# A hybrid decoder layer on one core: two lines for the second row of a pair, mLSTM steps further apart, weight parts shared evenly

## The chip, the core and the metric

The kernel runs on one core of a Trainium2 chip. The metric is the device time of one execution in microseconds; for the kernel before it is the median of three runs.

## What is computed

One inference step of a decoder layer, for a prompt of 2048 tokens (with 16 meta tokens in front) and for 8 samples of 8 tokens, with the same weights. All is float32. Cut to what matters here:

```python
def _in_proj(x, g_pre, w_in, b_in):
    h = _rmsnorm(x, g_pre)
    p = jnp.einsum('btd,dc->btc', h, w_in) + b_in
    return jnp.split(p, ...)          # qa ka va za qm km vm om zm im fm ga gb

def _mlstm_chunk(carry, inp):         # one chunk of 128 tokens, 4 heads of width 256
    Wqk = W * jnp.einsum('blhd,bshd->bhls', q, k)
    num = a[..., None] * jnp.einsum('blhd,bhde->bhle', q, C0) + jnp.einsum('bhls,bshe->bhle', Wqk, v)
    h = num / jnp.maximum(jnp.abs(den), jnp.exp(-m))[..., None]
    C1 = aL[..., None, None] * C0 + jnp.einsum('bshd,bshe->bhde', kw, v)

def _merge(x, att, hm, za, om, zm, ga, gb, w_pa, w_pb, w_out, g_post):
    y_a = att * jax.nn.silu(za)
    y_m = jax.nn.sigmoid(om) * hm * jax.nn.silu(zm)
    merged = jax.nn.sigmoid(ga) * (y_a @ w_pa) + jax.nn.sigmoid(gb) * (y_m @ w_pb)
    return x + _rmsnorm(merged @ w_out, g_post)
```

## The kernel before, in words

**Two stages.** A first stage (up to about 859 us) does the norm, the attention with its projections, and prepares data in DRAM. A barrier follows, and then `stream` runs all other projections; the change is in `stream` and in the last steps of the first stage.

**Passes, tiles, pairs.** `stream` goes through ten passes: ZM, H0 to H3 (one mLSTM head each: its q, k, o and v columns, and that head's mLSTM work), GA, PA, GB, PB and OUT. A pass multiplies 17 tiles of 128 tokens by a 1024x1024 weight. Tile 0 (meta and sample tokens) is a single one with four products; tiles 1 to 16 go in eight pairs (row 0 the odd tile, row 1 the even one) with seven products each, P1, P6, P5, P7, P2, P3, P4 in this order, on sums and differences of operands and of weight blocks (a scheme that saves one product in eight). So a pass has 60 products, and the program counts them through as q. A product is 12 matmuls of 128x512 (line 2760, 2762, 2763: each operand and weight is split into an upper and a lower float32r part). "Step" below is q within a pass, or within a pair from 0 to 6. Three PSUM banks serve all: `bank_x` is bank_first, `bank_y` bank_second, `bank_z` bank_third.

**Results and lines.** VectorE evicts the products (`evict_pair`) into lines of the tile `c`: row 0 of a pair has line 0, row 1 has line 1, the single tile line 2 (`line_of`). P7's eviction makes u3 and then the right half of row 1 (line 2497, semaphore c22), and P3, which uses the same bank, waits for c22. Before it writes into a line, VectorE waits in `wait_line` until the former tile has left it: its store to DRAM (ZM, GA, PA, GB), its mLSTM reads (head passes), its transposes (PB, `transposes`, line 2711), or its last addition (OUT: VectorE norms the row in `norm_row`, line 2555, and POOL adds x in `finish`, line 2215).

**mLSTM steps.** Tile n of a head is turned at q = `turned_at(n)` (TensorE transposes q and k, line 2783), scored one step later (L2792, with the transposes L2772 of the y of the tile before, `y_transposed`), mixed two steps later (L2808, L2809, L2812). ScalarE evicts the transposes (L2342), takes the exponential (L2333) and evicts y (L2379); VectorE makes mx_wqk (L2564) and mx_y (L2622). Tile 0 also does the samples' work inside the product of its mixing (`sample_rows`, L2839) and in the four after it (`state_update`).

**Weights.** A pass uses 28 weight parts ("units" of 128x512). SP loads each into one of `NW` = 6 waiting buffers (L2006), ScalarE makes the upper part (`upper_unit`, L2274), VectorE or POOL the lower (`lower_unit`, L2437 and L2177, `lower_by_dve` decides), two units a step from six steps ahead of a pass to its step 7. Differences of weight blocks for later passes are made on POOL (`differences`, L2184 to L2190) at steps fixed by `DIF_AT`; ScalarE's queue loads them three steps ahead (`load_dif`, L2262, which waits for the store of the one before last) and stores them three steps later (`store_dif`, L2266).

**Order.** Every engine runs a loop over q with its work written in a fixed order, and waits on semaphores. SP asks for the operand of product q + 3 at step q (L1636), and for a head's z four steps ahead of the turn (`load_z`, L2029, which waits for the gates of the tile two before).

## Time and profile before

| | before |
|---|---|
| runs, us | 2915.42, 2923.53, 2921.34 |
| median, us | 2921.34 |
| the profiled execution's own time, us | 2916.61 |
| its span, us | 2914.8 |
| TensorE busy | 2763.5 us, 95% |
| VectorE, ScalarE, POOL busy | 56%, 32%, 26% |
| granted clock of TensorE, mean | 0.979 |

The span runs from the first to the last instruction of one execution. TensorE's granted clock has two levels in the records, 1.00 (2.4 GHz) and 0.50 (1.2 GHz), and a stretch shows their mean. A list of waits says which engine's which line ended the idle time of TensorE; its idle time is the difference of span and busy time.

### The profile page before, as it was taken

The numbers are of one execution on the slowest core, as the hardware profiler recorded it, in microseconds if no ns is written. First come the engines' busy times: TensorE is split into PE (matmuls) and PEld (weight loads), VectorE is DVE, ScalarE is ACT, GpSimd is POOL, SyncE is SP. The second block draws the span as 40 slices with busy tenths as digits, with TensorE's granted clock in tenths as the row PEclk, the third lists the DMA queues.
The fourth block names the chain that finished last, engine by engine and source line by source line (L and its number), as shares of the span: only waits on it lengthen the run. The fifth ranks groups of instructions, "written<-read, shape, count | busy, mean of one in ns | idle before, by whom it ended". The sixth has DMA issues, their size and how long they took to land. (4 is left out here: it accounts for less than half of the span.)

```text
span 2914.8 us, 46458 instructions
## 1 busy us (share of the span) xinstructions
PE 2763.5 (95%) x15620; PEld 2298.4 (79%) x15620; DVE 1636.7 (56%) x4103; ACT 936.0 (32%) x2291; POOL 762.2 (26%) x1064
## 2 busy tenths in 40 slices
PE   6999999999999989999999998999999999999897
PEld 5888888888878768867877886888877878777676
DVE  5775665555652344464455455446256642677766
ACT  5774444444440021131132122113132321433432
POOL 3333534434540021131222223222000010223312
PEclk9999999999999999999999999999999999999999
DMA  8664565455777879887997997989795587856543
GB/s 301 241 214 160 178 210 196 166 176 191 233 232 233 299 250 301 295 305 236 286 309 260 283 284 254 283 278 308 246 304 171 184 301 252 297 186 215 188 147 116
DMA packets 410014, 697.47 MB, mean 239 GB/s; under 512 B 31778, under 2 KB 176551, under 8 KB 409748
## 3 DMA queue, kind: packets, MB, share of 16 engines
q1 hardware_dynamic: 298212, 526.72, 54.9%
q10 hardware_dynamic: 108848, 158.46, 16.1%
q0 software_dynamic: 2720, 9.32, 1.0%
q8 instruction: 128, 2.10, 0.3%
q14 instruction: 106, 0.87, 0.1%
HBM read 526.87 MB, written 169.48 MB: 239 GB/s over the span
## 5 line engine op out<-in xcount | busy, mean ns | idle before, releaser
L2760 PE MATMUL bank_second<-w_all,a_all 128*128 128x512 f32 x736 | 298.9, 406 | 2.0 <-DVE st_u L2491 0.9
L2763 PE MATMUL bank_second<-w_all,a_all 128*128 128x512 f32 x736 | 288.6, 392 | 0.0
L2762 PE MATMUL bank_second<-w_all,a_all 128*128 128x512 f32 x736 | 288.3, 392 | 0.0
L2177 POOL TENSOR_TENSOR w_all<-st_waiting,w_all 128x512 fp32r<-128x512 f32 x59 | 80.1, 1359 | 626.4 <-ACT w_all L2274 626.4
L2342 ACT ACTIVATE mx_qkt<-st_bank_t 128x512 f32<-128x512 f32 x68 | 40.7, 598 | 578.4 <-PE st_bank_t L2783 556.3
L2760 PE MATMUL bank_third<-w_all,a_all 128*128 128x512 f32 x464 | 190.3, 410 | 29.9 <-DVE st_c L2497 12.9
L2760 PE MATMUL bank_first<-w_all,a_all 128*128 128x512 f32 x496 | 197.5, 398 | 4.1 <-DMA a_all<-first_t 2.0
L2763 PE MATMUL bank_first<-w_all,a_all 128*128 128x512 f32 x496 | 194.6, 392 | 0.0
L2762 PE MATMUL bank_first<-w_all,a_all 128*128 128x512 f32 x496 | 194.6, 392 | 0.0
L2274 ACT ACTIVATE w_all<-st_waiting 128x512 fp32r<-128x512 f32 x188 | 111.7, 624 | 246.9 <-PE bank_first L2763 139.2
L307 PE MATMUL bank_first<-w_all,a_all 128*128 128x384 f32 x544 | 189.3, 348 | 0.0
L2184 POOL TENSOR_TENSOR h_raw<-h_raw 128x256 f32<-128x256 f32 x64 | 48.5, 757 | 538.4 <-DMA h_raw<-l_blocks_in 538.2
L2763 PE MATMUL bank_third<-w_all,a_all 128*128 128x512 f32 x464 | 184.6, 398 | 0.0
L2762 PE MATMUL bank_third<-w_all,a_all 128*128 128x512 f32 x464 | 184.4, 397 | 0.0
L309 PE MATMUL bank_first<-w_all,a_all 128*128 128x384 f32 x544 | 182.1, 335 | 0.0
L308 PE MATMUL bank_first<-w_all,a_all 128*128 128x384 f32 x544 | 182.0, 335 | 0.0
L917 ACT ACTIVATE at_sm<-at_sm,at_nmx 128x208 f32<-128x208 f32 x272 | 124.1, 457 | 154.1 <-DVE at_nmx L1138 154.1
L2760 PEld LDWEIGHTS bank_second<-w_all,a_all 128*128 128x128 f32 x736 | 139.6, 190 | 34.5 <-issue 6.8
L2763 PEld LDWEIGHTS bank_second<-w_all,a_all 128*128 128x128 f32 x736 | 139.1, 189 | 30.1
L2762 PEld LDWEIGHTS bank_second<-w_all,a_all 128*128 128x128 f32 x736 | 139.5, 190 | 26.8
L316 PE MATMUL bank_third<-w_all,a_all 128*128 128x256 f32 (+1 forms) x480 | 147.3, 307 | 0.2 <-POOL a_all L297 0.2
L2494 DVE TENSOR_TENSOR st_u<-bank_second,st_t 128x512 f32<-128x512 f32 x80 | 55.2, 690 | 157.3 <-PE bank_second L2763 157.3
(383 smaller groups left out, 7270.6 us busy)
## 6 DMA issues: line engine op xcount, KB each, us to landing
a_all<-sh_t SPq DMA_DIRECT2D x224, 512.0 KB, 5.0
a_all<-hh_t SPq DMA_DIRECT2D x180, 512.0 KB, 5.7
a_all<-hh_t ACTq DMA_DIRECT2D x104, 512.0 KB, 4.8
st_waiting<-difs_t SPq DMA_DIRECT2D x152, 256.0 KB, 6.3
h_raw<-l_blocks_in ACTq DMA_DIRECT2D x64, 512.0 KB, 5.7
difs_t<-h_raw ACTq DMA_DIRECT2D x64, 512.0 KB, 7.3
st_waiting<-l_blocks_in SPq DMA_DIRECT2D x108, 256.0 KB, 6.8
hh_t<-a_all SPq DMA_DIRECT2D x34, 512.0 KB, 6.2
```

Source lines behind the costliest of these rows:

```text
L307: nc.tensor.matmul(out, hi[:, j], k.w_hi[:, j, col:col + n], start=(j == 0), stop=False)
L308: nc.tensor.matmul(out, hi[:, j], k.w_lo[:, j, col:col + n], start=False, stop=False)
L309: last = nc.tensor.matmul(out, lo[:, j], k.w_hi[:, j, col:col + n], start=False, stop=(j == KT - 1))
L316: nc.tensor.matmul(out, hi[:, j], k.w_hi[:, j, col:col + n], start=(j == 0), stop=False)
L917: nc.scalar.activation(sm[:, g, :], sm[:, g, :], ACT.Exp, bias=nmx[:, g:g + 1], scale=HD ** -0.5, accum_out=rs[:, g:g + 1]).then_inc(exp_r ...
L2177: G.tensor_tensor(unit_half(v, 1), unit_view(v), unit_half(v, 0).bitcast(F32), ALU.subtract).then_inc(k.lower_done, 1)
L2184: G.tensor_tensor(d[:, R11], d[:, R12], d[:, R11], ALU.subtract).then_inc(dif_step, 1)
L2274: A.activation(unit_half(v, 0), unit_view(v), ACT.Copy).then_inc(k.upper_done, 1)
L2494: V.tensor_tensor(u3[:, :], bank_y[:, :], t2[:, :] if s in STREAMED else t1[:, :], ALU.add).then_inc(u3_ready, 1)
L2760: T.matmul(bank_view(bank, at), hi, weight_row(k, at, 0, t), start=fresh and t == 0, stop=False, skip_group_check=True)
L2762: T.matmul(bank_view(bank, at), hi, weight_row(k, at, 1, t), start=False, stop=False, skip_group_check=True)
L2763: last = T.matmul(bank_view(bank, at), lo, weight_row(k, at, 0, t), start=False, stop=t == KH - 1, skip_group_check=True)
```

## The change

`line_of` gives row 1 line 1 or 3 by turns, so `c` has four lines, and `former_item` looks two pairs back for row 1; the stores of lines 1 and 3 are counted apart (`stored_count`). In the output pass the norms come one step (row 0) and two steps (row 1) later. `turned_at` puts the turns of a head's tiles 0 to 5 at steps 7, 14, 17, 20, 22 and 25 (before: 4, 11, 12, 16, 18, 23) and those of later even tiles two steps later. `lower_by_dve` gives VectorE two of four lower parts in every pass, where it had three of four in the seven passes behind a streamed one. Four more units of the first pass are loaded in the first stage, into a part of `w_all` that is free then (`staged_unit`), and the ring of waiting buffers begins at `RING`. The semaphore for the right half of tile 0 in the first pass is now incremented by the first stage's own eviction.

```diff
--- before.py
+++ after.py
@@ -71,6 +71,7 @@
 PAIR_SLOTS = 5
+RING = EARLY + 4
@@ -352,6 +353,10 @@
     return k.w_all[:, :, KH * part + kt, 2 * LW:W_COLS]
+
+
+def staged_unit(k, v):
+    return k.w_plain[:, :, v % KH, 2 * LW:W_COLS]
 def unit_part(k, at, part, kt, n):
@@ -651,6 +656,8 @@
                         load_early(e)
+                    for v in range(EARLY, RING):
+                        sp.dma_start(staged_unit(k, v), unit_source(k, v).rearrange("p (i n) -> p i n", i=2)).then_inc(k.staged_in, 16)
                 if t == 0 and a + 1 < KVH:
@@ -1300,7 +1307,7 @@
             V.tensor_tensor(k.h_raw[:, 1, KH:KT].rearrange("p j n -> p (j n)"), k.bank_first[:, :],
-                            k.h_raw[:, 0, KH:KT].rearrange("p j n -> p (j n)"), ALU.add).then_inc(k.first_ready, 1)
+                            k.h_raw[:, 0, KH:KT].rearrange("p j n -> p (j n)"), ALU.add).then_inc(k.c12_ready, 1)
         @block.tensor
@@ -1657,7 +1664,7 @@
 def line_of(g, row):
-    return 2 if is_single(g) else row
+    return 2 if is_single(g) else (0, 1 + 2 * (pairs_before(g) % 2))[row]
 def row_turn(passes, g, row):
@@ -1665,16 +1672,21 @@
     return (N_ITEM - row) * passes.index(g // N_ITEM) + g % N_ITEM + 1 - row
-def stored_count(g):
-
-    n = STORING.index(g // N_ITEM)
-    return 16 * (n + 1 if is_single(g) else (N_ITEM - 1) * n + g % N_ITEM)
+def stored_count(g, row):
+
+    n, i = STORING.index(g // N_ITEM), g % N_ITEM
+    if is_single(g):
+        return 16 * (n + 1)
+    return 16 * ((N_ITEM - 1) * n + i) if row == 0 else 16 * ((N_ITEM - 1) // 2 * n + (i + 1) // 2)
 def former_item(g, row):
+    if row:
+        p = pairs_before(g) - 2
+        return N_ITEM * (p // (N_ITEM - 1)) + p % (N_ITEM - 1) + 1 if p >= 0 else None
     h = g - N_ITEM if is_single(g) else (g - 2 if is_single(g - 1) else g - 1)
-    return h if h >= 0 and row < len(tile_rows(h)) else None
+    return h if h >= 0 else None
 def turn_before(t):
@@ -1695,9 +1707,9 @@
     b = N_PROD * (H0 + h)
-    if t < 3:
-        return b + (4, 11, 12)[t]
-    return b + N_SINGLE + N_PAIR * (t // 2) + (5 if t % 2 else 0)
+    if t < 6:
+        return b + (7, 14, 17, 20, 22, 25)[t]
+    return b + N_SINGLE + N_PAIR * (t // 2) + (5 if t % 2 else 2)
 def scored_at(n):
@@ -1726,7 +1738,7 @@
         return v >= EARLY and kt % 2 == 1
-    return kt != 3 if s - 1 in STREAMED else kt % 2 == 1
+    return kt % 2 == 1
 def lower_counts(v):
@@ -1753,14 +1765,15 @@
     if s == 0:
-        return -4 if x < EARLY + NW else unit_split_at(v) - 1
+        return -4 if x < RING + NW else unit_split_at(v) - 1
     return N_PROD * (s - 1) + 46 + x if x < NW else unit_split_at(v) - 1
     SPLITS_AT.setdefault(unit_split_at(_v), []).append(_v)
-    LOADS_AT.setdefault(unit_loaded_at(_v), []).append(_v)
+    if _v >= RING:
+        LOADS_AT.setdefault(unit_loaded_at(_v), []).append(_v)
 def stream(nc, k):
@@ -1776,7 +1789,7 @@
         first = k.h_raw[:, 1].rearrange("p j n -> p (j n)")
-        c = sb("c", [P, 3, D + 1])
+        c = sb("c", [P, 4, D + 1])
         waiting = sb("waiting", [P, NW, LW])
@@ -1975,9 +1988,13 @@
         def unit_view(v):
-            return waiting[:, (v - EARLY) % NW].rearrange("p (i n) -> p i n", n=LW // 2 if slot_of(v) == 6 else P)
+            if v < RING:
+                return staged_unit(k, v)
+            return waiting[:, (v - RING) % NW].rearrange("p (i n) -> p i n", n=LW // 2 if slot_of(v) == 6 else P)
         def unit_half(v, part):
+            if v < RING:
+                return weight_row(k, slot_of(v), part, v % KH).rearrange("p (i n) -> p i n", i=2)
             return unit_part(k, slot_of(v), part, v % KH, P)
@@ -2161,8 +2178,9 @@
             sp.wait_ge(c_out[2], 16 * len(STORING))
-            for i in range(2):
-                sp.wait_ge(c_out[i], 16 * len(STORING) * (N_ITEM - 1))
+            sp.wait_ge(c_out[0], 16 * len(STORING) * (N_ITEM - 1))
+            for i in (1, 3):
+                sp.wait_ge(c_out[i], 16 * len(STORING) * (N_ITEM - 1) // 2)
             sp.wait_ge(shift_out, 32)
@@ -2268,7 +2286,12 @@
             def upper_unit(v):
-                act.wait_ge(unit_in[(v - EARLY) % NW], 16 * ((v - EARLY) // NW + 1))
+                if v < RING:
+                    act.wait_ge(k.staged_in, 16 * KH)
+                else:
+                    act.wait_ge(unit_in[(v - RING) % NW], 16 * ((v - RING) // NW + 1))
+                if v == RING:
+                    wait_unit(act, RING - 1)
                 if unit_free(v):
@@ -2457,7 +2480,6 @@
                 if g == 0 and j == 1:
-                    dve.sem_inc(c12_ready, 1)
                     return
@@ -2494,7 +2516,7 @@
                     dve.wait_ge(u3_ready, m + 1)
-                    V.tensor_tensor(c[:, 1, LW:D], bank_z[:, :], u3[:, :], ALU.add).then_inc(c22_ready, 1)
+                    V.tensor_tensor(c[:, line_of(g, 1), LW:D], bank_z[:, :], u3[:, :], ALU.add).then_inc(c22_ready, 1)
                 elif j == P2:
@@ -2691,7 +2713,7 @@
                 for row in range(2):
-                    g = ended(q - 1 - 2 * row, row)
+                    g = ended(q - 2 - 3 * row, row)
                     if g is not None and g // N_ITEM == OUT:
...
```

Left out are the places where names follow (`EARLY` to `RING` in `load_unit`, `stored_count` with a row, `c[:, 1, ...]` to `c[:, line_of(g, 1), ...]` for the left half, a fourth semaphore of `c_out`).

TensorE in the second head pass (H1), between the last matmul of a product and the first of the next; st_bank_t<-ident,st_c is a turn, st_bank_s<-ident,mx_y the transposes of the y before, st_bank_n<-mx_qkt a score, and st_bank_n<-mx_cn, st_bank_n<-st_c and st_bank_u a mixing. Before, steps 12 to 14:

```order
L2763 MATMUL bank_second<-w_early,a_all 128x512
L2783 MATMUL st_bank_t<-ident,st_c 128x128 x4
L2772 MATMUL st_bank_s<-ident,mx_y 128x128 x2
L2792 MATMUL st_bank_n<-mx_qkt 128x128 x2
L2760 MATMUL bank_third<-w_all,a_all 128x512
...
L2763 MATMUL bank_third<-w_all,a_all 128x512
L2808 MATMUL st_bank_n<-mx_cn,mx_qat 128x257 x2
L2809 MATMUL st_bank_n<-st_c,mx_wqk 128x257
L2812 MATMUL st_bank_u<-st_c,mx_kw 128x257 x2
L2772 MATMUL st_bank_s<-ident,mx_y 128x128 x2
L2792 MATMUL st_bank_n<-mx_qkt 128x128 x2
```

And now, steps 14 to 17:

```order
L2785 MATMUL bank_second<-w_all,a_all 128x512
L2805 MATMUL st_bank_t<-ident,st_c 128x128 x4
...
L2785 MATMUL bank_first<-w_all,a_all 128x512
L2794 MATMUL st_bank_s<-ident,mx_y 128x128 x2
L2814 MATMUL st_bank_n<-mx_qkt 128x128 x2
...
L2785 MATMUL bank_third<-w_all,a_all 128x512
L2830 MATMUL st_bank_n<-mx_cn,mx_qat 128x257 x2
L2831 MATMUL st_bank_n<-st_c,mx_wqk 128x257
L2834 MATMUL st_bank_u<-st_c,mx_kw 128x257 x2
L2782 MATMUL bank_second<-w_all,a_all 128x512
```

Before, the transposes of tile 1's y stood directly behind its mixing; now a product stands between a mixing and the next transposes.

VectorE in a pair of the output pass, from the eviction of P6 on. Before:

```order
L2491 TENSOR_TENSOR st_u<-bank_second,st_t 128x512
L2432 TENSOR_TENSOR a_all<-h_raw,a_all 128x512
L2432 TENSOR_TENSOR a_all<-st_raw,a_all 128x512
L2553 RECIPROCAL st_small<-st_small 128x1
L2555 SCALAR_TENSOR_TENSOR st_c<-st_c,st_small,st_e 128x1024
L2494 TENSOR_TENSOR st_u<-bank_second,st_t 128x512
L2497 TENSOR_TENSOR st_c<-bank_third,st_u 128x512
```

And now:

```order
L2513 TENSOR_TENSOR st_u<-bank_second,st_t 128x512
L2455 TENSOR_TENSOR a_all<-h_raw,a_all 128x512
L2575 RECIPROCAL st_small<-st_small 128x1
L2577 SCALAR_TENSOR_TENSOR st_c<-st_c,st_small,st_e 128x1024
L2455 TENSOR_TENSOR a_all<-st_raw,a_all 128x512
L2516 TENSOR_TENSOR st_u<-bank_second,st_t 128x512
L2519 TENSOR_TENSOR st_c<-bank_third,st_u 128x512
```

The norm ahead of P7's eviction was that of row 1; now it is that of row 0, and the norm of row 1 follows P2's eviction.

POOL at the start of PB (st_c<-st_c,st_e is the addition of the single tile, st_e<-pa_t the load for the next). Before:

```order
L2198 DMA st_e<-pa_t 128x1024 x2
L2177 TENSOR_TENSOR w_all<-st_waiting,w_all 128x512
L2177 TENSOR_TENSOR w_early<-st_waiting,w_early 128x512
L2209 TENSOR_TENSOR st_c<-st_c,st_e 128x1024
L2198 DMA st_e<-pa_t 128x1024
L2177 TENSOR_TENSOR w_all<-st_waiting,w_all 128x512
L2177 TENSOR_TENSOR w_all<-st_waiting,w_all 128x2x256
```

And now:

```order
L2216 DMA st_e<-pa_t 128x1024 x2
L2195 TENSOR_TENSOR w_all<-st_waiting,w_all 128x512 x2
L2195 TENSOR_TENSOR w_early<-st_waiting,w_early 128x512 x2
L2195 TENSOR_TENSOR w_all<-st_waiting,w_all 128x512
L2227 TENSOR_TENSOR st_c<-st_c,st_e 128x1024
L2216 DMA st_e<-pa_t 128x1024
L2195 TENSOR_TENSOR w_all<-st_waiting,w_all 128x512
L2195 TENSOR_TENSOR w_all<-st_waiting,w_all 128x2x256 x2
```

POOL has one more weight part directly ahead of the addition, and twice as many in all.

## Rows read from the trace of the kernel before

**Rows 1.** Busy time by engine, from the page, and the clock by core.

```profile
PE 2763.5 (95%) x15620; PEld 2298.4 (79%) x15620; DVE 1636.7 (56%) x4103; ACT 936.0 (32%) x2291; POOL 762.2 (26%) x1064
...
core 0: 2914.8 us, clock 0.979
```

**Rows 2.** TensorE's waits: who ended them, us in total, times, longest.

```profile
PE bank_third L2760 <- DVE st_c L2497: 27.4, 21, 3.4
PE st_bank_s L2772 <- ACT mx_yt L2379: 12.5, 4, 3.1
...
PE st_bank_n L2839 <- DVE mx_wqk L2564: 10.0, 4, 4.9
...
PE st_bank_n L2808 <- DVE mx_wqk L2564: 4.8, 3, 3.9
...
PE st_bank_n L2792 <- ACT mx_qkt L2342: 3.9, 2, 3.6
...
PE st_bank_t L2783 <- DVE st_c L2465: 2.2, 2, 1.3
```

**Rows 3.** Stretches: us, busy PE, PEld, DVE, ACT, POOL, clock, DMA, GB/s.

```profile
2765.70:2787.20 21.50, 19.55 (x84) 15.64 (x85) 15.43 (x22) 7.58 (x14) 4.77 (x2) 1.00 0.45 147
2787.20:2810.30 23.10, 21.19 (x85) 16.77 (x85) 15.41 (x22) 7.59 (x14) 4.75 (x2) 0.93 0.40 137
...
1337.00:1345.00 8.00, 7.49 (x30) 6.49 (x31) 1.90 (x6) 0.94 (x4) 0.06 (x1) 0.79 0.83 284
...
1045.00:1062.00 17.00, 13.90 (x65) 7.30 (x64) 7.94 (x16) 7.69 (x17) 7.21 (x8) 0.80 0.83 290
...
2162.00:2172.00 10.00, 9.55 (x35) 7.78 (x36) 8.87 (x14) 6.88 (x12) 2.65 (x2) 0.83 0.93 318
```

**Rows 4.** Timeline of VectorE and TensorE in a pair of the output pass.

```profile
2809.45 0.69 DVE L2497 TENSOR_TENSOR st_c<-bank_third,st_u 128x512 f32<-128x512 f32 x1 [1.88 <-POOL st_e L2215]
...
2810.29 0.47 PE L2760 MATMUL bank_third<-w_early,a_all 128*128 128x512 f32 x1 [1.91 <-DVE st_c L2497]
```

**Rows 5.** TensorE's waits from 2702.4 us on, and from 2536 to 2702.4 us.

```profile
PE bank_third L2760 <- DVE st_c L2497: 12.2, 7, 1.9
...
PE bank_third L2760 <- DVE st_c L2497: 6.1, 7, 0.9
```

**Rows 6.** Timeline at tile 1's mixing in H1.

```profile
1335.77 0.48 DVE L2622 SCALAR_TENSOR_TENSOR mx_y<-st_bank_n,mx_den,mx_tz 128x256 f32<-128x256 f32 x1
...
1337.51 0.66 PE L2772 MATMUL st_bank_s<-ident,mx_y 128*128 128x128 f32 x2 [3.11 <-ACT mx_yt L2379]
```

**Rows 7.** Timeline of ScalarE at the start of H1.

```profile
1283.72 1.15 ACT L2274 ACTIVATE w_early<-st_waiting 128x512 fp32r<-128x512 f32 x2 [6.19 <-DMA difs_t<-h_raw]
...
1295.11 0.31 ACT L2333 ACTIVATE mx_wexp<-mx_wexp 128x128 f32<-128x128 f32 x1 [4.25 <-DMA difs_t<-h_raw]
```

**Rows 8.** 1024 to 2010 us: a wait of SP, and operand loads (count, KB, median us to landing).

```profile
SPq L2029 <- DVE mx_tz L2595: 58.4, 11, 9.7
...
a_all<-hh_t SPq DMA_DIRECT2D x107, 512.0 KB, 5.7
```

**Rows 9.** TensorE's waits from 855 to 975 us.

```profile
PE bank_third L2760 <- DMA a_all<-sh_t: 3.6, 1, 3.6
```

**Rows 10.** Lower parts on POOL: count, busy us, mean ns, idle before.

```profile
L2177 POOL TENSOR_TENSOR w_all<-st_waiting,w_all 128x512 fp32r<-128x512 f32 x59 | 80.1, 1359 | 626.4 <-ACT w_all L2274 626.4
```

**Rows 11.** Timeline at the starts of PB and of the output pass.

```profile
2527.78 2.45 POOL L2209 TENSOR_TENSOR st_c<-st_c,st_e 128x1024 f32<-128x1024 f32 x1
...
2530.29 1.11 PE L2711 MATMUL st_bank_t<-ident,st_c 128*128 128x128 f32 x4 [1.33 <-POOL st_c L2209]
...
2733.83 1.74 DVE L2437 TENSOR_TENSOR w_all<-st_waiting,w_all 128x512 fp32r<-128x512 f32 x1
...
2730.97 2.38 POOL L2215 TENSOR_TENSOR st_e<-st_c,st_e 128x1024 f32<-128x1024 f32 x1 [3.95 <-DVE st_c L2555]
2733.32 3.39 POOL L2177 TENSOR_TENSOR w_all<-st_waiting,w_all 128x512 fp32r<-128x512 f32 x2
```

More of the change, by code:

```diff
@@ L726, in _ @@
                 load_operand(sp, k, q)
-            sp.wait_ge(k.first_ready, 1)
+            sp.wait_ge(k.c12_ready, 1)
             sp.wait_ge(scan_out, 48)
@@ L1823, in stream @@
         t1_ready, t2_ready, u2_ready, u3_ready = sem("t1_ready"), sem("t2_ready"), sem("u2_ready"), sem("u3_ready")
-        c11_ready, c12_ready, c21_ready, c22_ready = sem("c11"), sem("c12"), sem("c21"), sem("c22")
-        c_out = [sem(f"c_out{i}") for i in range(3)]
+        c11_ready, c12_ready, c21_ready, c22_ready = sem("c11"), k.c12_ready, sem("c21"), sem("c22")
+        c_out = [sem(f"c_out{i}") for i in range(4)]
         out_done = [sem("out_done0"), sem("out_done1")]
@@ L1940, in wait_line @@
             if s in STORING:
-                eng.wait_ge(c_out[at], stored_count(h))
+                eng.wait_ge(c_out[at], stored_count(h, row))
             elif s in HEAD_PASSES:
@@ L2026, in load_z @@
                 if h == 0:
-                    row = 2 if t == 0 else 1 - t % 2
-                    sp.wait_ge(c_out[row], stored_count((t + 1) // 2))
+                    row = 0 if t == 0 else 1 - t % 2
+                    sp.wait_ge(c_out[line_of((t + 1) // 2, row)], stored_count((t + 1) // 2, row))
                 sp.dma_start(z[:, n % 2], k.zm_t[t, :, h * MD:(h + 1) * MD]).then_inc(z_in[n % 2], 16)
@@ L2048, in load_e @@
                 else:
-                    sp.wait_ge(c_out[line_of(g, row)], stored_count(g - N_ITEM))
+                    sp.wait_ge(c_out[line_of(g, row)], stored_count(g - N_ITEM, row))
                     sp.dma_start(e[:, row], (k.ga_t if s == PA else k.gb_t)[t]).then_inc(e_in[row], 16)
```

10 lines of the change are left out of this document (5 added, 5 removed).

## The prediction

> **What bounds the kernel now.** The page comes first. TensorE is busy for 2763.5 of 2914.8 us and no other engine passes 56% [rows 1], so only what makes TensorE wait, or slows its clock, can be worth anything. The list of TensorE's waits then gives the targets [rows 2]: 27.4 us in 21 waits for the VectorE line L2497, and five kinds that belong to the mLSTM steps of the head passes: 12.5 (L2379), 10.0 and 4.8 (L2564), 3.9 (L2342), 2.2 (L2465), together 33.4 us. Third, the clock. The granted clock falls right behind such waits: a stretch of 8 us that begins with the 3.1 us wait at 1337 us was granted 0.79, and (1 - 0.79) x 8 is 1.7 us lost on top of the wait [rows 3]. In the output pass a pair without a drop lasts 21.5 us at clock 1.00, one with a drop 23.1 us at 0.93 [rows 3]; of the five pairs from 2765.7 to 2877.8 us, three are of the second kind. I take 1.65 us for each drop.
>
> **Second row in two lines.** L2497 writes the right half of row 1 into its line as soon as P7, the fourth of the seven products, is done, and TensorE's P3 waits for that, because both use bank_third. Before, the line has one copy, so L2497 also waits until row 1 of the pair before has left it. The output pass shows it: VectorE sits idle for 1.88 us until POOL's addition (L2215) is done, runs L2497 at 2809.45, and TensorE starts P3 at 2810.29 after 1.91 us [rows 4]. With two lines the copy that L2497 needs was left a whole pair (19.6 us) earlier. There are 12.2 us of these waits in the output pass, 6.1 us in PB, where the line is held by the transposes of the row before [rows 5], and the remaining 9.1 of the 27.4 in ZM, GA and GB, where a store holds it. The two lines remove the whole 27.4. Four drops follow such waits, the three in the output pass and one in GA, at 2162 us, with 0.83 over 10 us [rows 3]: 4 x 1.65 = 6.6. Term: -34.0.
>
> What is late next in the output pass? The norms move one and two steps back. VectorE works 15.4 us in each pair of 21.5 [rows 3], so it fits a pair of 19.6 us (84 matmuls, about 0.23 us from start to start). Row 0 keeps one line, but that is rewritten only in step 5 of the next pair (steps counted from 0), and its norm in step 2 leaves three steps, 8 us, for the norm and POOL's 2.38 us [rows 11]. I cost that at nothing.
>
> **mLSTM steps spread out.** The steps themselves stay; only their places change. Tiles 1 and 2 were turned in adjacent steps, so the transposes of tile 1's result came straight behind its own mixing. VectorE makes mx_y only at 1335.77, ScalarE's L2379 comes behind it, and TensorE, which has nothing else in its order, waits 3.11 us [rows 6]. In the new order a product of 2.7 us or more lies between each mixing and its transposes, as in the rest of the pass, where no such wait is seen. The four waits (12.5) go and their drops (four, 6.7): -19.2.
>
> The other kinds, 20.9 us, come from ScalarE and VectorE lagging at the change of pass, plus one double drop (17 us at 0.80 is 3.4 [rows 3]) and three single ones behind the longest waits of H1, H2 and H3 (3 x 1.7): 29.4 in all. Here I give only half. The trace shows that ScalarE isn't late through the weight parts alone: at 1295.11 the exponential (L2333) had waited 4.25 us for a store of differences, since the load of the next differences (L2262) stands ahead of it and waits for that store; at 1283.72 a weight part had waited 6.19 us in the same way [rows 7]. These loads keep their steps (DIF_AT is unchanged), and the mLSTM steps move into others of them. Their period is 18 steps for 5 loads against 60 a pass. Counting it out, a load stands in step 3 of H1 (where tile 16 of the head before is now evicted by ScalarE), in steps 4 and 8 of H2, in step 9 of H3 (exponential of tile 0). So H0, and tile 0 of H1, should be freed, and H2, H3 and the start of H1 keep something. Term: -14.7 (bounds: -29.4 if all go, +10 if a wait of 5 us comes up twice more than now).
>
> The denser steps also touch SP. A load of z at four steps ahead waits for the gates of the tile two before; where turns stand 5 steps apart (17 and 22, 20 and 25, 22 and 27) SP now waits one step, with operand loads queued behind it. SP already does so in 11 places, 58.4 us in total, up to 9.7 [rows 8], and no operand came late for it. An operand is asked for three products ahead, some 9 to 12 us with the mLSTM work between, and lands in 5.7 us [rows 8]; a delay near 3 us fits. Cost: nothing, or 1 us at each of 16 places if it doesn't.
>
> **First pass.** Before, six unit loads stand in front of the first operand load on SP, and TensorE waits 3.6 us for an operand [rows 9]. Four of the ten units now come earlier, so four loads (about 1.0 us less issue, 0.5 MB less in front) remain. Not all of the wait goes; -3.0 with a little clock (bounds 0 and -8). The four loads now stand on SP ahead of the last stores of the first stage, 4 x 0.5 us, and TensorE is still in its products then: nothing. The semaphore that replaces the early increment gives 0.2 us at most.
>
> **Lower parts shared evenly.** 49 of 196 parts move from VectorE to POOL, where one takes 1359 ns [rows 10]. At a pass start that is one in each step of 2.7 us, so POOL keeps up, except where it has other work in its queue. That is PB: POOL adds the single tile (2.45 us), and TensorE's transposes at 2530.29 have waited 1.33 us for it [rows 11]. In the new order one more part stands ahead of the add and the third part of T1, which was VectorE's, behind it: 2 x 1.36 = +2.7 us. In the output pass the share doesn't change, but the norm of row 0 of the first tile does: it stands in front of POOL's add (2.38 us at 2730.97), and that in front of POOL's parts at 2733.32, the first of which TensorE waits for [rows 11]. One step later on VectorE puts an eviction (0.69) and a split ahead of the norm, which I take together as +1.9, with POOL slowing the split. Sum +4.6 (bounds 0 and +12).
> POOL's work also slows VectorE beside it: L2437 took 1.74 us while POOL made its parts [rows 11], against 0.69 us for an instruction of the same size with POOL idle [rows 4]. The Trainium skill (GPSIMD Engine Reference, Specifications) says that GpSimd shares its SBUF interfaces with VectorE and contends with instructions of two SBUF inputs, which speaks against this share; the trace agrees by the 1.74 against 0.69. If every part on POOL delayed a VectorE instruction that TensorE waits for once per pass start, seven starts x 1.05 would be +7; VectorE is busy 56% of the span [rows 1], and I leave it at 0.
>
> **Sum.** -34.0 - 19.2 - 14.7 - 3.0 + 4.6 = -66.3 us. Against the profiled execution (2916.6 us, span 2914.8): 2850.3. That execution lies 4.7 under the median of 2921.34, so the same difference puts the median at 2855.0.
>
> **Rivals.**
> (a) The wait of the output pass comes back at another gate (row 0's single line, or the later norm and POOL). For it: the chain norm, add, store, load is serial. Against: 15.4 us of VectorE in 21.5. Price: 12.2 + 3 x 1.65 = 17 back, 2872. Chance 0.08.
> (b) The difference loads meet the moved steps at every pass start, so nothing of the second part of the head waits is gained, or more waits than before. For it: the waits of ScalarE [rows 7] and the count above. 14.7 back is 2870, with five further waits of 3 us 2885. Chance 0.17.
> (c) Slower: SP's waits for the gates make operands late. It decides where an operand's load, issued some 3 us late, takes over 8 us as it does near pass starts, at 16 places. To lose 66 us and more, each would have to cost 3 us and a drop with it: 16 x 4.7 = 75, 2930. Against it: the 58.4 us SP already waits without one late operand in these steps. Chance 0.04.
> (d) The moved waits stay as they are: TensorE's order changes but the waits (c22 of row 1, or the transposes of y) turn up in front of the next instruction, because something else than the named one, a DMA landing at the same time, ended them. Then only a few us go: 2912 to 2925. Chance 0.04.
>
> **Numbers.** My forecast has 0.67. Its own range is 2838 to 2868. Down: the other half of the head waits (-14.7) and the first pass (-5) give 2835, nearly the low end; up: its own upper end takes +13 for the bounds of the starts of PB and the output pass (+7) and six of the 1 us waits behind SP. With (a) and (b) it reaches 2884, so 2834 to 2884 leaves out (c), (d) and part of (b), and some of the forecast's own cases, under 2 in 10 together. A measurement tells 0.3% (9 us) from no change. Faster by more than that: 0.67 + 0.08 + 0.17 = 0.92, of which I move 0.01 to slower for what I may have missed; within: 0.04 (d); slower: 0.04 + 0.01 = 0.05.
>
> **What would show it.** Right: no wait of P3 for L2497's successor, output-pass pairs near 19.6 us at clock 1.00, no wait of the y transposes for mx_yt, a granted clock over the whole above 0.985 (0.979 now [rows 1]). Remaining waits at starts of H1, H2 and H3 should be ended by ScalarE or wqk with a difference load ahead on ScalarE. TensorE's waits for POOL's w_all or POOL's add at the start of PB and of the output pass should have grown by 2 to 3 us each. Wrong: new waits for a_all operands in head passes (c), for the row 0 eviction in the output pass (a).

## The result, and the profile after

The changed kernel takes 2873.86 us (median of four runs, 2868.58 to 2875.27), the kernel before, run beside it, 2918.78 (four runs, 2915.42 to 2923.53). The ratio is 0.9842, 95% interval 0.9821 to 0.9862: 1.6% faster, 44.9 us. Forecast were 2855.0 and 66.3 us. The sign was right, and 2873.86 lies in the stated range of 2834 to 2884, but above the 2838 to 2868 that the forecast's own terms allowed: the part between comes from rivals (a) and (b). The gain was forecast half again as large as it is.

The page and the clock after:

```profile
PE 2746.9 (96%) x15620; PEld 2291.3 (80%) x15620; DVE 1642.8 (57%) x4054; ACT 938.2 (33%) x2291; POOL 834.4 (29%) x1113
...
core 0: 2871.5 us, clock 0.986
```

Against [rows 1]: 49 instructions have gone from VectorE to POOL, as the share says, and the mean granted clock rose from 0.979 to 0.986. TensorE's waits after (who ended them, us in total, times, longest), to be laid beside [rows 2]:

```profile
PE st_bank_n L2830 <- DVE mx_wqk L2586: 7.5, 4, 2.7
...
PE bank_third L2782 <- POOL w_early L2195: 4.6, 3, 3.4
...
PE bank_third L2782 <- DVE st_c L2519: 4.4, 4, 1.5
PE st_bank_t L2733 <- POOL st_c L2227: 4.3, 2, 3.5
PE bank_second L2782 <- DMA a_all<-sh_t: 4.0, 2, 3.1
PE st_bank_n L2814 <- ACT mx_qkt L2365: 3.3, 1, 3.3
...
PE st_bank_n L2861 <- DVE mx_wqk L2586: 1.7, 1, 1.7
```

The wait for the right half of row 1 fell from 27.4 us in 21 waits to 4.4 in 4 (L2497 is L2519 now), and the transposes of y (12.5 us in 4) are gone from the list. New are the 3.4 us for a POOL part and the 3.1 for an operand; the longest one for POOL's addition grew from 1.3 to 3.5.

The passes one by one, worked out from the trace: a pass begins with the first matmul of its first product; "waits" sums TensorE's idle time in it, "half clock" is the time granted 0.50. OUT is counted to its last product; some 11 us of norms and stores follow. ZM's waits include the one ahead of its first product (2.0 and 3.2 us).

| pass | us before | us after | waits before, after | half clock before, after |
|---|---|---|---|---|
| ZM | 164.7 | 159.9 | 8.6, 7.5 | 10.2, 3.4 |
| H0 | 240.9 | 243.7 | 9.1, 12.3 | 13.7, 10.2 |
| H1 | 243.4 | 237.6 | 9.3, 4.6 | 6.8, 3.4 |
| H2 | 242.0 | 238.0 | 7.9, 4.8 | 6.8, 3.4 |
| H3 | 242.9 | 239.5 | 8.7, 6.0 | 6.8, 3.4 |
| GA | 176.3 | 171.0 | 4.4, 0.9 | 3.4, 0.0 |
| PA, GB | 339.8 | 341.1 | 9.2, 10.0 | 3.4, 3.4 |
| PB | 193.1 | 186.6 | 11.0, 5.5 | 6.8, 6.8 |
| OUT | 200.8 | 181.2 | 22.9, 11.8 | 23.9, 10.2 |

The span fell by 43.3 us, the passes together by 45.3 (`stream` begins 2.3 us later in the trace after). Waits fell by 27.6 (91.1 to 63.5), and half clock by 37.5 (81.9 to 44.4), which at half speed is 18.7 us of work: 46.3 together, within 3 us of either fall. So the books close, and four tenths of the gain is clock. What fell short is the heads: four passes, 10.4 us for the 33.9 forecast, and H0 even grew.

### The profile page after: what moved, and what is told of

Its sections match the earlier page's. It is cut to its first block, busy times and chain, and to the rows that moved or that the text cites. A ratio compares the mean times of both kernels' runs of the same rounds, so it can differ in the third digit from the quotient of the medians.

```text
span 2871.5 us, 46433 instructions
## 1 busy us (share of the span) xinstructions
PE 2746.9 (96%) x15620; PEld 2291.3 (80%) x15620; DVE 1642.8 (57%) x4054; ACT 938.2 (33%) x2291; POOL 834.4 (29%) x1113
## 4 chain that ended last, share of the span: by engine, by line
PE 56%; DMA 8%; DVE 2%; issue 2%; SPq 1%; POOL 1%; ACT 1%; POOLq 0%; ACTq 0%; DVEq 0%
PE bank_second L2782 7%; PE bank_second L2785 7%; PE bank_second L2784 7%; PE bank_third L2782 5%; PE bank_first L2782 5%; PE bank_third L2785 5%; PE bank_third L2784 5%; PE bank_first L2785 5%; PE bank_first L2784 4%; DMA st_waiting<-l_blocks_in 2%; DMA st_waiting<-difs_t 2%; PE st_bank_u L2834 2%; PE st_bank_n L2830 2%; DMA a_all<-hh_t 1%; DMA a_all<-sh_t 1%
## 5 line engine op out<-in xcount | busy, mean ns | idle before, releaser
L2195 POOL TENSOR_TENSOR w_all<-st_waiting,w_all 128x512 fp32r<-128x512 f32 x92 | 128.7, 1405 | 576.3 <-ACT w_all L2297 576.1
L2782 PE MATMUL bank_third<-w_all,a_all 128*128 128x512 f32 x464 | 192.3, 414 | 23.8 <-POOL w_all L2195 12.3
L2516 DVE TENSOR_TENSOR st_u<-bank_second,st_t 128x512 f32<-128x512 f32 x80 | 55.1, 689 | 158.7 <-PE bank_second L2785 158.7
```

The source lines that it names most:

```text
L2195: G.tensor_tensor(unit_half(v, 1), unit_view(v), unit_half(v, 0).bitcast(F32), ALU.subtract).then_inc(k.lower_done, 1)
L2782: T.matmul(bank_view(bank, at), hi, weight_row(k, at, 0, t), start=fresh and t == 0, stop=False, skip_group_check=True)
```

## Experiments

Each kernel ran beside the kernel before, whose median in the five groups of runs was 2917.2 to 2922.7. Differences under 9 us (0.3%) between two versions aren't told apart by the times; for those the passes and waits in the traces have to speak, one execution each. They vary too: H2 takes 238.0, 236.4 and 240.4 us in the changed kernel and in experiments 4 and 5, whose edits don't touch it, and its wait at step 4 is 1.69, 3.30 and 4.31 us. The start of `stream` varies by 6 (856.7 to 862.9 in all the versions), so for close versions its length from there on ("the stream", 2009.8 us in the changed kernel, 2055.4 before) is compared as well.

**1. The two lines alone** (the kernel before, with the second line for row 1 and the counts that follow from it; only the semaphore of tile 0 in the first pass is also that of the changed kernel). Its edit against the kernel before, cut to the main line:

```diff
 def line_of(g, row):
-    return 2 if is_single(g) else row
+    return 2 if is_single(g) else (0, 1 + 2 * (pairs_before(g) % 2))[row]
```

Expected: 

> The kernel before with the two lines for the second row alone (old steps, old share, old norms, no unit loaded early). Theory: the lines carry the 34.0 us of the first term (27.4 us of waits, 6.6 of clock), and the rest little: 2884 against 2917 of the kernel before, output pass 182 to 184 us in place of 200.8, PB 186 to 187 in place of 193.1. Rival: the lines need the later norms to work, since the norm of row 1 stood in a full step: output pass 190 us or more, 2892 or more.

Measured: 2891.07 us (2885.52 to 2892.19, six runs), ratio 0.9901 [0.9883, 0.9919]: 30.5 us under its kernel before. The L2519 wait is down to 2.4 us in two waits, OUT takes 183.7 us, PB 185.0, GA 170.1. So the lines bring two thirds of the whole gain by themselves. In its list of TensorE's waits the kinds of the heads stand as in [rows 2]:

```profile
PE st_bank_s L2794 <- ACT mx_yt L2402: 12.4, 4, 3.1
PE st_bank_n L2861 <- DVE mx_wqk L2586: 11.5, 4, 5.3
```

**2. The old turns** (the changed kernel, with tiles turned as before):

```diff
-    if t < 6:
-        return b + (7, 14, 17, 20, 22, 25)[t]
-    return b + N_SINGLE + N_PAIR * (t // 2) + (5 if t % 2 else 2)
+    if t < 3:
+        return b + (4, 11, 12)[t]
+    return b + N_SINGLE + N_PAIR * (t // 2) + (5 if t % 2 else 0)
```

Expected: 

> The changed kernel with the old steps of the mLSTM work. Theory: the four waits of 3.1 us for mx_yt come back with four drops (19.2 us), the waits at tile 0 come back, and the new ones of the changed kernel (3.1 us with a double drop in H0 for an operand, 3.3 in H1) go: 12 us slower, 2886. Rival: spreading them gave nothing in the sum, since the differences on ScalarE and the waits on SP took it back: 2870 to 2877.

Measured: 2890.52 us (2889.52 to 2892.25), 0.9911 [0.9896, 0.9925]. The new turns are worth 16.7 us, not 33.9; the four head passes give 17.7 (976.5 against 958.8). The four waits come back in full, with the drop behind each; timeline of TensorE at tile 1's mixing in H1 (start, us, engine, line, operation, tiles; in brackets the idle time before):

```profile
1339.24 0.41 PE L2794 MATMUL st_bank_s<-ident,mx_y 128*128 128x128 f32 x2 [3.11 <-ACT mx_yt L2402]
...
1342.68 0.63 PE L2784 MATMUL bank_second<-w_all,a_all 128*128 128x512 f32 x1
...
1344.04 0.40 PE L2785 MATMUL bank_second<-w_all,a_all 128*128 128x512 f32 x1
```

The matmuls behind the wait last 0.63 us and start every 0.43, later ones 0.40 and every 0.23. This is the same place and the same 3.11 us as in [rows 6]. H1 to H3 take 734.0 us against 715.1 with the new turns, but H0 242.5 against 243.7: H0 is where the new turns gave nothing.

**3. The old share of the lower parts:**

```diff
-    return kt % 2 == 1
+    return kt != 3 if s - 1 in STREAMED else kt % 2 == 1
```

Expected: 

> The changed kernel with the old share of lower weight parts (VectorE three of four behind a streamed pass). Theory: the even share costs, through POOL's queue: the 3.4 us wait of H0 for a part that stands behind differences on POOL, with its clock drop (1.7), and one part ahead of the addition at the start of PB (1.8 or more). Without it about 7 us faster than the changed kernel's 2873.9: 2867. Rival: VectorE was the late engine at the starts of the passes and the share relieves it: 3 to 8 us slower, 2877 to 2882, with more waits for mx_wqk.

Measured: 2867.4 us (2864.78 to 2870.36), 0.9831 [0.9816, 0.9846]: 6.5 us less than the changed kernel, near the 7 expected, but inside 0.3%, and the traces don't bear it out: the stream takes 2009.1 us against 2009.8, and nearly all of the difference of the two profiled executions is that `stream` begins 5.0 us earlier (856.7 against 861.7), which this edit doesn't reach. So what the share costs in all is open. Where it costs shows in POOL's timeline of the changed kernel at step 6 of H0:

```profile
1043.65 1.27 POOL L2195 TENSOR_TENSOR w_early<-st_waiting,w_early 128x512 fp32r<-128x512 f32 x1 [2.62 <-ACT w_early L2297]
1044.87 1.18 POOL L2202 TENSOR_TENSOR h_raw<-h_raw 128x256 f32<-128x256 f32 x1
...
1047.75 1.19 POOL L2208 TENSOR_TENSOR h_raw<-h_raw 128x256 f32<-128x256 f32 x1
1048.90 1.26 POOL L2195 TENSOR_TENSOR w_early<-st_waiting,w_early 128x512 fp32r<-128x512 f32 x1
```

and TensorE's next matmul there:

```profile
1050.21 0.51 PE L2782 MATMUL bank_third<-w_early,a_all 128*128 128x512 f32 x1 [3.44 <-POOL w_early L2195]
```

A part that TensorE needs next stands behind the four differences, 4 us of POOL's work. With the old share the wait there is 0.86 us, on VectorE, and the one of the transposes at the start of PB 1.44 us instead of 3.47. VectorE takes most of it back: TensorE's list has 7.7 us in six waits for VectorE's parts of `w_all` (1.3 in three after), 3.0 of them at step 6 of PB, right behind the shorter wait for the addition.

**4. The old norms:**

```diff
-                    g = ended(q - 2 - 3 * row, row)
+                    g = ended(q - 1 - 2 * row, row)
```

Expected: 

> The changed kernel with the norms of the output pass in their old steps (row 0 one step, row 1 two steps earlier), and with the two lines kept. Theory: the lines alone took the waits away, the later norm only delays POOL's addition at the start of the output pass, where the wait for POOL is 6.3 us (4.9 before): 1.5 to 2 us faster than 2873.9, pairs of the output pass still 19.2 to 19.6 us. Rival: the norms in their old, full steps delay VectorE, P3 waits again for the eviction of P7, 0.5 us and more in each of seven pairs: 2877 or more.

Measured: 2870.31 us (2864.98 to 2880.59), 0.9852 [0.983, 0.9874], not told from the changed kernel. Two effects are seen in the traces. At the start of OUT TensorE waits 4.90 us for POOL instead of 6.25, as forecast. But a steady pair gets longer. Stretches of one pair (us, busy PE, PEld, DVE, ACT, POOL, clock, DMA share, GB/s), first the changed kernel, then this one:

```profile
2727.30:2746.30 19.00, 19.00 (x85) 15.76 (x84) 15.63 (x21) 7.58 (x14) 3.74 (x2) 1.00 0.28 108
```

```profile
2715.20:2734.90 19.70, 19.57 (x86) 15.65 (x85) 16.23 (x21) 7.59 (x14) 4.77 (x2) 1.00 0.34 105
```

There are six such steady pairs, 19.04 us each against 19.65 to 19.68, some 3.8 us together, and OUT takes 183.9 us against 181.2. The kernel of experiment 1, with the norms at the old steps too, also has pairs of 19.7. So the later norms earn 0.6 us a pair and cost 1.35 at the start; I had them at nothing and 1.9.

**5. The old ring** of the first pass:

```diff
-RING = EARLY + 4
+RING = EARLY
```

Expected: 

> The changed kernel without the four units of the first pass that are loaded in the first stage. Theory: the step over the barrier falls from 3.2 to about 2.0 us wait, as before the change, and the wait for the operand of the first pair rises from 2.3 to 3.6 us with a double clock drop instead of a single one (+1.7): together 1 to 2 us slower, 2875, not to be told from 2873.9. Rival: the early loads carry the whole gain of the first pass (4.8 us there): 2878.

Measured: 2873.89 us (2868.21 to 2876.99), 0.9851 [0.9835, 0.9867], equal to the changed kernel. In the trace ZM takes 165.4 us against 159.9 (158.6 to 162.3 in all others with the new ring, 163.8 and 164.7 in the other two without), so the pass did gain 4 to 5 us. The whole stream is 3.8 us longer without the new ring (2013.6), and that isn't told from the scatter. The gain is seen in a pass only, and 3.0 was a fair term.

**6. Difference loads later** (ScalarE's load behind the mLSTM work of its step):

```diff
-                if q + 3 in DIF_NOW:
-                    load_dif(DIF_NOW[q + 3])
                 if q - 3 in DIF_NOW:
                     store_dif(DIF_NOW[q - 3])
                 mixer_first(q)
                 if q + 3 < Q_ALL:
                     split_operand(q + 3)
                 mixer_second(q)
+                if q + 3 in DIF_NOW:
+                    load_dif(DIF_NOW[q + 3])
```

Expected: 

> The changed kernel with ScalarE's load of the next differences behind that step's mLSTM evictions and exponential, not ahead of them. Theory: the waits that the changed kernel keeps in step 3 of H1 (3.3 us for mx_qkt), step 4 of H2 (1.7) and step 9 of H3 (1.7, both for mx_wqk) come from ScalarE standing at this load until the store of the one before last has landed; they go with one or two clock drops: 6.7 us of waits and 3 us of clock, 10 us faster, about 2864. Rival: ScalarE is late for the weight parts, whose units land late; then the three waits stay within 1 us of what they are, 2874.

In the changed kernel ScalarE's transposed tile at step 3 of H1 shows what is to be tested; its timeline, and TensorE's next matmul in its own:

```profile
1283.28 0.60 ACT L2365 ACTIVATE mx_qkt<-st_bank_t 128x512 f32<-128x512 f32 x1 [5.55 <-DMA difs_t<-h_raw]
```

```profile
1283.93 1.23 PE L2814 MATMUL st_bank_n<-mx_qkt 128*128 128x128 f32 x4 [3.26 <-ACT mx_qkt L2365]
```

Measured: 2869.89 us (2865.91 to 2871.28), 0.9828 [0.9808, 0.9848]; 2864 was expected. The 3.26 us wait is gone, but one of 2.66 (step 4) and one of 2.21 (step 9) for mx_wqk stand in H1 instead; H2's wait at step 4 is gone, H2's and H3's at step 0 (2.06, 1.89) stay. For the wait of step 3 the cause holds, the remedy doesn't: the load that waits for a store now holds up the weight parts and the exponential of step 4 (ScalarE waits 3.83 us for it there) instead of the transposed tile. The waits of step 0 look to have another cause, see below.

**7. The window copies in H3.** The wait for an operand at step 28 of H0 had not been expected from any count of SP's waits alone. SP's timeline there, in the changed kernel:

```profile
1125.50 0.33 SPq L2046 DMA_DIRECT2D mx_z<-zm_t  x1
...
1128.04 0.80 SPq L2118 DMA_DIRECT2D o_s_wk<-cache_win_k_in  x1
1128.87 0.74 SPq L2118 DMA_DIRECT2D o_s_wv<-cache_win_v_in  x1
1129.66 0.44 SPq L1643 DMA_DIRECT2D a_all<-sh_t  x1
...
1137.05 0.33 SPq L2046 DMA_DIRECT2D mx_z<-zm_t  x1
```

and SP's wait from 1118 to 1126 us:

```profile
SPq L2046 <- DVE mx_tz L2617: 6.1, 1, 6.1
```

SP stands 6.1 us before the load of z until 1125.50. Then come an operand load, two copies within DRAM, 960 KB each, and at 1129.66 the operand load for step 28. It lands 14.6 us later, at 1144.30, and TensorE has waited for it; its clock falls:

```profile
1144.35 0.80 PE L2782 MATMUL bank_second<-w_all,a_all 128*128 128x512 f32 x1 [3.09 <-DMA a_all<-sh_t]
```

```profile
1142.00:1152.00 10.00, 7.65 (x24) 6.18 (x25) 2.63 (x7) 1.48 (x5) 2.91 (x4) 0.66 0.75 269
```

(1 - 0.66) x 10 is 3.4 us beside the 3.1. SP's next stop before z, until 1137.05, begins when this load is long out, so it has no part in this wait. The load behind the copies, issued at 1129.66 us in the changed kernel and at 1135.87 in the kernel before (count, KB, us to landing), and SP's and TensorE's rows of the kernel before:

```profile
a_all<-sh_t SPq DMA_DIRECT2D x1, 512.0 KB, 14.6
```

```profile
a_all<-sh_t SPq DMA_DIRECT2D x1, 512.0 KB, 12.8
```

```profile
1135.87 0.37 SPq L1636 DMA_DIRECT2D a_all<-sh_t  x1
```

```profile
1149.83 0.58 PE L2760 MATMUL bank_second<-w_all,a_all 128*128 128x512 f32 x1
```

So the landing was slow before the change too. But there the lead, the time from the issue until TensorE is ready for the operand, was 14.0 us, enough for 12.8; after the change TensorE is ready 11.6 us after the issue (1144.35 less the wait of 3.09), too little for 14.6. Of the 2.4 us less, 1.1 are SP's (it issues 0.7 us behind the first matmul of step 25, before 0.4 ahead of it) and 1.2 the steps 25 to 27, in which less mLSTM work lies now.

The edit:

```diff
-                    if h == 0 and x == 24:
+                    if h == 3 and x == 40:
```

Expected: 

> The changed kernel with the two copies of the window caches (960 KB each, DRAM to DRAM) issued in step 40 of H3 in place of step 24 of H0. Theory: the wait of 3.1 us for an operand in step 28 of H0, with its double clock drop, needs the slow landings (12 us) behind these copies as well as SP's wait for the gates; without the copies the landing is 5 to 6 us and the wait is gone: 3.1 + 3.4 = 6.5 us faster, 2867. Rival: SP's wait for the gates is enough by itself: the wait in step 28 stays at 2 us or more, and 2872 to 2874.

Measured: 2867.68 us (2864.48 to 2869.29), 0.9821 [0.9801, 0.9841], near the 2867 expected, but the wait moved instead of going, so the reason given is only half right. H0 falls from 243.7 to 235.5 us and its wait is gone; H3 grows from 239.5 to 245.0, with this in its list of waits:

```profile
PE bank_third L2782 <- DMA a_all<-sh_t: 3.5, 1, 3.5
```

The wait follows the copies.

**8. z and the gate rows asked for two steps later:**

```diff
-                t = TURN.get(q + 4)
+                t = TURN.get(q + 2)
```

The load of z then stands nearer to its turn, where the gates of the tile two before are ready.

Expected: 

> The changed kernel with the loads of z and of the rows asked for two steps ahead of a turn, not four, so that SP no longer stands behind the gates (now 91.8 us in 20 waits in the head passes, 58.4 in 11 before). Theory: the operand loads behind them go out in time, the wait in step 28 of H0 (3.1 us, double drop) and those of 1.0 us and less in step 36 of H1 and H2 go: 8 us faster, 2866, unless z itself comes late for ScalarE. Rival: it is the copies alone that slow the operand's landing: step 28 keeps its wait, 2873.

Measured: 2872.11 us (2871.45 to 2875.75), 0.984 [0.982, 0.986]; 2866 was expected. SP's waits in the heads (1024 to 2010 us) hold 91.8 us for the gates in the changed kernel, against 58.4 before [rows 8]:

```profile
SPq L2046 <- DVE mx_tz L2617: 91.8, 20, 6.2
```

With the edit this line is gone, and so is the wait at step 28 of H0, copies and all: the operand load behind them still takes 13.6 us, but goes out 13.9 us before step 28. So that wait needs both, the copies and SP standing still ahead of them. But operand waits of 1.2, 2.1 and 2.6 us stand at step 36 of H0, H1 and H2 (none, 0.4 and 1.0 without the edit), and the time stays.

**9. No copies at all** (the two are left out, so the shifted part of the two window outputs isn't written):

```diff
-                    if h == 0 and x == 24:
-                        for dst, src in ((k.o_s_wk, k.cache_win_k), (k.o_s_wv, k.cache_win_v)):
...
-            sp.wait_ge(shift_out, 32)
```

Expected: 

> The changed kernel without the two copies of the window caches (they are left out, so the shifted part of the two window outputs isn't written). Theory (the operand wait of 3.1 us at step 28 of H0 and its drops need the copies, and so does the one of 3.5 us that turned up in H3 when they stood there): no operand wait over 1.5 us in any head pass, H0 in 236 to 238 us instead of 243.7, all other passes unchanged, time 2867. Rival (SP's waits for the gates alone make operands late, the copies only pick the place): a wait of about 3 us remains in a head pass, time 2872 to 2875.

Measured: 2867.86 us (2861.25 to 2869.76), 0.9802 [0.9785, 0.9818]. No operand wait over 1.5 us in a head pass except at H0's first products (2.4 at step 1), H0 238.5 us, H1 to H3 within 1 us of the changed kernel, and the load for step 28 lands after 5.8 us. In the changed kernel the copies cost 5 us in H0 (6.0 by the times, inside 0.3%), and this is what can be had from placing them well.

**10. Old share, copies in step 30 of GA**, where SP waits for no gates:

```diff
-                    if h == 0 and x == 24:
+                if s == GA and x == 30:
```

Expected: 

> The changed kernel with the former share of the lower parts and with the copies of the window caches in step 30 of GA, where SP waits for no gates. Theory (both costs are separate: the POOL part at step 6 of H0 and the start of PB about 6 us; the copies about 6 us, and in GA they cost nothing because SP is never late there): 2862, both savings added, H0 near 235 us, GA within 1 us of 171. Rival (the copies make operands late wherever they stand): GA grows by 3 to 6 us with an operand wait in steps 30 to 36, time 2867. Rival (the separate gains overlap, since one wait in H0 only takes the place of another): 2867 to 2870, with H0 at 238 or more.

Measured: 2869.83 us (2868.84 to 2872.1), 0.9817 [0.9802, 0.9831]. The first rival came true: H0 is down to 233.7 us, but GA grew from 171.0 to 179.8. Operand loads issued from 2057 to 2070 us (count, KB, median us to landing), and GA's only wait of TensorE from its start to 2122 us:

```profile
a_all<-sh_t SPq DMA_DIRECT2D x3, 512.0 KB, 12.1
```

```profile
PE bank_third L2782 <- DMA a_all<-sh_t: 5.0, 1, 5.0
```

A product lasts 2.7 us here with no mLSTM work between. The load right behind the copies goes out 8.1 us before TensorE is ready for it and lands after 13.1: late by 5.0, without any wait of SP's. In the heads of the kernel before the same lead was 14.0 us, which is why it got away with it.

**11. The same, with the old norms and the later difference loads.**

Expected: 

> As best_a, with the norms of the output pass back at their former steps and ScalarE's loads of the differences placed behind the mLSTM work of their step. Theory (each of the two took some 3 us off alone: POOL's wait at the start of the output pass 6.3 to 4.9, and the 3.3 us wait of H1 for mx_qkt): 2857, 5 us under best_a. Rival (the single gains of 3 to 4 us were mostly spread between runs): same as best_a within 3 us, 2862.

Measured: 2867.24 us (2862.23 to 2873.86), 0.9808 [0.9788, 0.9828]; GA 179.5 again. The rival came true: not told from experiment 10. The head passes are the shortest of all, 943.6 us against 958.8 after.

**12. The same, with the copies cut into 16 pieces** over steps 12 to 42 of GA:

```diff
-                if s == GA and x == 30:
-                    for dst, src in ((k.o_s_wk, k.cache_win_k), (k.o_s_wv, k.cache_win_v)):
+                if s == GA and 12 <= x < 12 + 4 * NB and x % 2 == 0:
+                    dst, src = ((k.o_s_wk, k.cache_win_k), (k.o_s_wv, k.cache_win_v))[(x - 12) // 2 % 2]
+                    b = (x - 12) // 4
```

Expected: 

> As best_b, but the two copies of the window caches cut into 16 (one sample's keys or values each, an eighth of a copy), one at every second step from 12 to 42 of GA. Theory (a whole copy makes operand loads land after 12 to 13 us for some 10 us, so TensorE waits 5 us once wherever it stands; an eighth every 5.4 us only lifts each landing a little, and an operand has 8 us): GA in 172 instead of 179.5 us, no operand wait over 1.5 us between its steps 12 and 46, time 2860. Rival (the copies cost their bytes, not their burst): several operand waits near 1 us in GA, GA at 176 to 180, time 2865 to 2868.

Measured: 2862.9 us (2855.37 to 2874.16), 0.9806 [0.9779, 0.9833]. GA takes 170.4 us and has no wait of TensorE from its start to 2102 us. Loads issued from 2007 to 2090 us:

```profile
a_all<-sh_t SPq DMA_DIRECT2D x17, 512.0 KB, 5.0
a_all<-hh_t SPq DMA_DIRECT2D x13, 512.0 KB, 5.8
...
o_s_wv<-cache_win_v_in SPq DMA_DIRECT2D x8, 120.0 KB, 5.8
```

The same bytes in small pieces, and operands land after 5 us as if there were none. This has the lowest median, 11 us under the changed kernel, but its runs spread over 19 us and the intervals overlap, so "faster than the change" is likely, not shown; what the traces show is GA, 9 us shorter than with whole copies.

## Why the prediction was right in sign and too large

Term by term, in the order of the prediction; "time" is from the medians, "trace" from passes.

| term | forecast | measured |
|---|---|---|
| two lines | -34.0 | -30.5 (time, 1) |
| y transposes and their drops | -19.2 | all four waits gone |
| other waits of the heads | -14.7 | together with the row above -16.7 (time, 2), so about +2.5 |
| first pass | -3.0 | about -5 in the pass, 0 in the time (5) |
| even share (start of PB) | +2.7 | +6.5 by the time (inside 0.3%), +0.7 by the stream (3) |
| later norms | +1.9 | +1.35 at the start, -3.8 in the pairs (trace, 4) |
| sum | -66.3 | -44.9 |

**Two lines: right.** 25 of the 27.4 us of waits went in experiment 1, pairs of the output pass came to 19.7 us with the lines alone and to 19.0 at clock 1.00 with the later norms (19.6 forecast), and nothing stood in for the wait, so rivals (a) and (d) did not come true.

**The y transposes: right.** Each of the four waits went with its drop, and each came back in experiment 2.

**The other waits of the heads: this step failed, and it is most of the miss (17 us).** It read: the steps move away from the late engines at the change of pass, so half of 29.4 us goes. The list did shrink: 20.9 us of waits to 12.5 (7.5, 3.3 and 1.7), and with three drops behind them (5.1 us, 8.5 before) the 29.4 us came to 17.6. That is 11.8 gained for the 14.7 booked. But the step booked only the waits that could leave, at places of their own, and nothing for what the moved work would meet. Two things took their place in H0: a POOL part behind the differences (3.44 and a drop, 5.1 us) and the operand at step 28 (3.09 and 3.4 of clock, 6.5 us), together as much as had been gained, with five waits of 0.9 to 1.7 us for operands in steps 1 to 6 of H0, where one of 2.05 had been. The first needs the even share as well: it is 3.1 to 3.4 us in all seven traces with new turns and even share, and 0.9 us, on VectorE, with the old share (3). This is the time of rival (b), "14.7 back is 2870", but its mechanism, the difference loads, accounts for only part: in experiment 6 moving them moved the waits.

Of the 12.5 us, 6.6 are where the count put them: step 3 of H1 (mx_qkt, 3.26), step 4 of H2 (mx_wqk, 1.69), step 9 of H3 (1.66), each with a difference load ahead on ScalarE that waits for its store. The other 5.8 are at step 0 of H1, H2 and H3 (0.99, 2.11, 2.74), at the mixing of tile 15, which didn't move; the step gave no place for them. There ScalarE had waited 2.93 us (H2) and 1.99 (H3) for the load of a weight part that stands ahead of the exponential, and VectorE has a weight part and an eviction ahead of mx_wqk; none of that is a difference load, which fits that experiment 6 left them. What would take them away wasn't tried.

**SP's waits at no cost: wrong in one place.** The argument was that SP already waited 58.4 us without a late operand, and that a delay near 3 us fits beside a landing of 5.7. Both rows spoke of the heads as a whole, a total and a median. The delay was no larger than thought (2.4 us less lead), but the one load right behind 1.9 MB of copies took 14.6 us to land, and had taken 12.8 of its 14.0 us already before. It is rival (c) at 1 of its 16 places. The copies stood in the code, unchanged, and in SP's order of work; the step never looked at what else is in the queue. Price: some 5 us in H0 (experiment 9).

**Even share: a place was missed; the size is open.** I counted where POOL has its additions (PB, OUT) and wrote that it keeps up "except where it has other work in its queue", but took the differences, 4 us of POOL at fixed steps, for no such work. TensorE's waits for POOL are 2.0 us longer at PB and 3.4 instead of 0.9 at step 6 of H0, while 6.4 us of waits for VectorE's parts are saved. Whether the sum is nearer to 0.7 or to 6.5 us these runs can't tell.

**First pass: right to within 2 us. Norms: +1.9 for about -2.5**, since that the pairs would get 0.6 us shorter was not seen.

Of the 21 us between 66.3 and 44.9, the heads are 17 and the lines 3.5. The other rows are smaller than the times tell apart and partly cancel. The rows are single medians and traces, good to a few us each, so this shows where the gain went, not each to the microsecond. That the time stayed in the stated range is in part luck: the range was wide enough on the slow side only because rivals (a) and (b) had been added to it, and neither came true as described.

## What to carry to other kernels

A second buffer pays in full what its waits cost, and its drops of the clock too: here 25 us of waits in 19 places gave 30 us. When steps are moved, don't subtract only the waits that they had; go through the steps into which they move and list, for each queue, what stands there already (other engines' fixed work, bulk copies, loads that wait for stores), since the moved work meets these one at a time. Bulk copies that nobody waits for can be cut into pieces between the loads that matter; here pieces of 120 KB cost nothing that shows.

## What was not expected of the hardware

**The load behind two whole copies within DRAM stands behind all their bytes.** In the twelve traces with the two copies of 960 KB in one step, the next operand load of 512 KB landed after 12.7 to 15.3 us, against 5.8 for the same load without them (experiment 9). The 7 to 10 us more are about what 1.9 MB take at the 290 GB/s that DMA moved in that stretch of experiment 10 (an estimate, nearly 7 us), and some. The same bytes as 16 pieces of 120 KB, one each 5.4 us, left the operand loads at 5.0 and 5.8 us (experiment 12).

**VectorE's splits last up to four times as long beside POOL's work.** Timelines of VectorE and POOL in the output pass, after:

```profile
2755.50 2.62 DVE L2455 TENSOR_TENSOR a_all<-st_raw,a_all 128x512 fp32r<-128x512 f32 x1 [0.40 <-ACT a_all L2270]
...
2758.05 0.68 DVE L2516 TENSOR_TENSOR st_u<-bank_second,st_t 128x512 f32<-128x512 f32 x1
```

```profile
2755.18 2.40 POOL L2233 TENSOR_TENSOR st_e<-st_c,st_e 128x1024 f32<-128x1024 f32 x1 [7.83 <-DVE st_c L2577]
```

Over the whole trace 115 splits (L2455) with POOL idle take 0.69 us on average, the 62 that overlap work of POOL 1.49, up to 2.62. Instructions with one input from PSUM aren't touched: L2516 takes 0.69 us beside POOL (16) and without (64). The Trainium skill (GPSIMD Engine Reference, Specifications) says that GpSimd shares SBUF interfaces with VectorE and contends with its instructions of two SBUF inputs; the trace agrees. That a slower VectorE hides behind TensorE, as I had assumed, holds in the output pass: its pairs run at 19.0 us with a busy TensorE.

**Waits of one length cost the clock or not.** Between the first products of `stream` and the start of the output pass, TensorE has 19 waits of 2.0 to 4.9 us in the traces before and after, and behind each the granted clock fell to 0.50, worth 1.7 us of work, or twice that. Yet of the six waits of 1.86 to 1.91 us in the steady output pairs before, three had a fall and three none. In all fourteen traces this stretch has 53 waits of 2.0 to 3.0 us: behind 34 the clock fell, 16 had no fall, and 3 stood in a drop that was already running. Of 68 waits of 3 us and more 66 had a fall; the two without were 3.42 us (step 28 of H0, experiment 6) and 3.30 us (step 4 of H2, experiment 4). So the two traces with which this began are more regular than the rest: here a drop went with nearly every wait of 3 us and more, and with two in three of those between 2 and 3.
